# A two-layer attention trunk with its layer loop written out: layer 0 reads the input itself, and the final norm moves into the last merge stage

## The reference, cut to what matters

```python
def rms_norm(x, w):
    y = x * rsqrt(mean(x * x, axis=-1) + EPS)
    return y * w

def mixer_layer(x, ...):
    h = rms_norm(x, norm_w)
    u = h @ w_in                       # 1024 -> 6144 columns: q, k, v, gates of two branches, merge gates
    ...                                # differential attention (o_da), stick-breaking attention (o_sb)
    y_da = (rms_norm(o_da, subln_w) * (1.0 - lam_init)) * silu(gd)
    y_sb = o_sb * silu(gs)
    merged = sigmoid(ga) * (y_da @ w_proj_da) + sigmoid(gb) * (y_sb @ w_proj_sb)
    return x + merged @ w_out, (kd, vd, ks, vs)

for l in range(2):
    x, rows = mixer_layer(x, ...)
y = rms_norm(x, final_norm_w)          # outputs: y and the new k and v rows of each layer
```

## Time and profile before

| what | us |
|---|---|
| median of 3 runs (lowest, highest) | 3524.44 (3505.21, 3526.84) |
| the profiled execution | 3517.19 |
| its span, first to last instruction | 3515.4 |
| PE busy | 2985.0 (85% of the span) |
| DVE busy / ACT busy | 1558.3 / 992.9 |
| mean granted PE clock, as a share of full speed | 0.924 |

### The profile page before, as it was taken

One profiled execution on the slowest core, in us unless ns is written; L12 is line 12 of the kernel. 1 busy time (PEld: TensorE's weight loads), 2 busy tenths in 40 slices (PEclk: granted clock), 3 DMA queues, 4 the chain that ended last, 5 costly groups with the idle time before them and its releaser, 6 DMA issues. The chain is left out here.

```text
span 3515.4 us, 52769 instructions
## 1 busy us (share of the span) xinstructions
PE 2985.0 (85%) x19664; PEld 2303.6 (66%) x19664; DVE 1558.3 (44%) x2399; ACT 992.9 (28%) x1751; POOL 0.2 (0%) x4
## 2 busy tenths in 40 slices
PE   5999999787787877769889999997877788786896
PEld 4888888555555555558668888884555555555685
DVE  4522110355664746564263222105646557455543
ACT  3101111343443524320030011113525344343211
POOL 0000000000000000000000000000000000000000
PEclk9999999898998989879989999998979889897998
DMA  4322221664544554354242222116555554553444
GB/s 174 141 96 88 79 95 51 218 215 166 184 168 164 206 187 153 110 200 139 93 153 102 96 95 96 72 48 233 207 177 172 202 180 162 190 183 117 170 139 160
DMA packets 288645, 516.62 MB, mean 147 GB/s; under 512 B 19040, under 2 KB 89824, under 8 KB 282208
## 3 DMA queue, kind: packets, MB, share of 16 engines
q1 hardware_dynamic: 288432, 513.72, 42.0%
HBM read 433.43 MB, written 84.93 MB: 147 GB/s over the span
## 5 line engine op out<-in xcount | busy, mean ns | idle before, releaser
L185 PE MATMUL A_acc<-A_w_hi,A_ht_hi 128*128 128x512 f32 x1728 | 675.2, 391 | 5.9 <-DVE A_w_lo L326 5.9
L185 PE MATMUL A_acc<-A_w_hi,A_ht_lo 128*128 128x512 f32 x1728 | 673.5, 390 | 0.0
L185 PE MATMUL A_acc<-A_w_lo,A_ht_hi 128*128 128x512 f32 x1728 | 673.3, 390 | 0.0
L719 PE MATMUL B_tr<-ident,B_k 128*128 128x128 f32 x2048 | 325.9, 296 | 123.9 <-DVE B_ckt L954 111.5
L719 PEld LDWEIGHTS B_tr<-ident,B_k 128*128 128x128 f32 x2048 | 232.7, 148 | 270.5 <-DVE B_ckt L954 138.8
L185 PEld LDWEIGHTS A_acc<-A_w_hi,A_ht_hi 128*128 128x128 f32 x1728 | 325.1, 188 | 73.8 <-issue 6.6
L185 PEld LDWEIGHTS A_acc<-A_w_hi,A_ht_lo 128*128 128x128 f32 x1728 | 325.0, 188 | 67.9
L185 PEld LDWEIGHTS A_acc<-A_w_lo,A_ht_hi 128*128 128x128 f32 x1728 | 325.2, 188 | 67.1
L801 PE MATMUL B_ov<-B_nat_v,B_wt 128*128 128x64 f32 (+1 forms) x1728 | 239.9, 297 | 0.0
L954 DVE COPY B_ckt<-B_tr 128x512 f32<-128x512 f32 x272 | 186.8, 687 | 104.2 <-PE B_tr L719 103.9
L801 PEld LDWEIGHTS B_ov<-B_nat_v,B_wt 128*128 128x128 f32 x1728 | 232.5, 215 | 0.0
(11 more groups left out here) (140 smaller groups left out, 3559.5 us busy)
## 6 DMA issues: line engine op xcount, KB each, us to landing
B_k<-in_cache_da_k SPq DMA_DIRECT2D x64, 1024.0 KB, 5.4
B_v<-in_cache_da_v SPq DMA_DIRECT2D x64, 1024.0 KB, 9.9
B_k<-in_cache_sb_k SPq DMA_DIRECT2D x64, 1024.0 KB, 5.2
B_v<-in_cache_sb_v SPq DMA_DIRECT2D x64, 1024.0 KB, 9.5
A_w_raw<-in_w_in SPq DMA_DIRECT2D x48, 1024.0 KB, 5.3
tmp_gates<-A_stage SPq DMA_DIRECT2D x72, 256.0 KB, 2.0
D_gate<-tmp_gates SPq DMA_DIRECT2D x72, 256.0 KB, 3.5
D_w_raw<-in_w_merge SPq DMA_DIRECT2D x32, 512.0 KB, 6.3
```

The lines of the kernel that those rows point to most:

```text
L185: last = nc.tensor.matmul(acc[:, i % RING, :], h[:, k, t * P:(t + 1) * P], w[:, b, k, :], start=(n == 0), stop=(n == 3 * KC - 1))
L719: last = nc.tensor.transpose(tr[:, r % 2, j * P:(j + 1) * P], block_, ident[:, :])
```

## The change

The diff with the renaming of tiles and semaphores (from "A_" to f"A{l}_" and so on, in all three phases) left out:

```diff
 def end_phase(nc, sems):
-    nums = [s.num for s in sems]
-    assert max(nums) - min(nums) == len(nums) - 1
-    nc.gpsimd.sem_clear(range(min(nums), max(nums) + 1))
+    nums = sorted(s.num for s in sems)
+    first = nums[0]
+    for num, after in zip(nums, nums[1:] + [None]):
+        if after != num + 1:
+            nc.gpsimd.sem_clear(range(first, num + 1))
+            first = after
     nc.all_engine_barrier()

+def x_of(dram, l):
+    return dram["x_all"] if l == 0 else dram["x"]

 # phase_project, SP
-                sp.wait_ge(const["x_here0"], 16)
                 for t in range(2):
-                    sp.dma_start(x_in[:, t, :], dram["x"][t]).then_inc(x_sems[t], 16)
+                    sp.dma_start(x_in[:, t, :], x_of(dram, l)[t]).then_inc(x_sems[t], 16)
                 load_w(0, True)
-                sp.wait_ge(const["x_here1"], 16)
                 for t in range(2, NT):
                     sp.wait_ge(S["hn_ready"], t - 1)
-                    sp.dma_start(x_in[:, t % 2, :], dram["x"][t]).then_inc(x_sems[t % 2], 16)
+                    sp.dma_start(x_in[:, t % 2, :], x_of(dram, l)[t]).then_inc(x_sems[t % 2], 16)

 # phase_merge
+        final = l == DEPTH - 1
+        fw = sbuf(f"D{l}_fw", [P, D])
+        fsq = sbuf(f"D{l}_fsq", [P, D])
+        fstats = sbuf(f"D{l}_fstats", [P, 4])
 # SP
                 def load_x(i):
                     done(sp, "x_ready", i - 1)
-                    sp.dma_start(x_in[:, :], dram["x"][i - 1]).then_inc(S["in1"], 16)
+                    sp.dma_start(x_in[:, :], x_of(dram, l)[i - 1]).then_inc(S["in1"], 16)
                 def store_x(i):
-                    sp.wait_ge(S["x_ready"], i)
-                    sp.dma_start(dram["x"][i - 1], x_out[:, :]).then_inc(S["x_stored"], 16)
+                    if final:
+                        sp.wait_ge(S["y_out"], i)
+                        sp.dma_start(dram["y"][i - 1], x_out[:, :]).then_inc(S["x_stored"], 16)
+                    else:
+                        sp.wait_ge(S["x_ready"], i)
+                        sp.dma_start(dram["x"][i - 1], x_out[:, :]).then_inc(S["x_stored"], 16)
                         ...
+                if final:
+                    sp.dma_start(fw[:, :], dram["final_norm_w"]).then_inc(S["fw_in"], 16)
                 load_branches(3)
                 load_gates(2)
 # ACT
+                def final_norm(i):
+                    act.wait_ge(S["x_ready"], i)
+                    done(act, "fsq_done", i - 1)
+                    nc.scalar.activation(fsq[:, :], x_out[:, :], ACT.Square, accum_out=fstats[:, 0:1]).then_inc(S["fsq_done"], 1)
+                    act.wait_ge(S["fvar_ready"], i)
+                    nc.scalar.activation(fstats[:, 2:3], fstats[:, 1:2], ACT.Sqrt).then_inc(S["fsd_ready"], 1)
                 with act.Fori(2, NT) as i:
                     root(i + 1)
                     y_part(i + 1)
                     m_part(i)
+                    if final:
+                        final_norm(i - 1)
                 m_part(NT)
+                if final:
+                    final_norm(NT - 1)
+                    final_norm(NT)
 # DVE
+                def final_norm(i):
+                    dve.wait_ge(S["fsq_done"], i)
+                    nc.vector.tensor_scalar(fstats[:, 1:2], fstats[:, 0:1], 1.0 / D, EPS, ALU.mult, ALU.add).then_inc(S["fvar_ready"], 1)
+                    dve.wait_ge(S["fsd_ready"], i)
+                    nc.vector.reciprocal(fstats[:, 3:4], fstats[:, 2:3]).then_inc(S["f_step"], 1)
+                    dve.wait_ge(S["f_step"], i)
+                    nc.vector.scalar_tensor_tensor(out=x_out[:, :], in0=x_out[:, :], scalar=fstats[:, 3:4], in1=fw[:, :],
+                                                   op0=ALU.mult, op1=ALU.mult).then_inc(S["y_out"], 1)
+                if final:
+                    dve.wait_ge(S["fw_in"], 16)
                 with dve.Fori(2, NT) as i:
                     ...
                     m_part(i)
+                    if final:
+                        final_norm(i - 1)
                 merge(NT)
                 add_x(NT - 1)
                 m_part(NT)
+                if final:
+                    final_norm(NT - 1)
                 add_x(NT)
+                if final:
+                    final_norm(NT)

-def phase_final(nc, dram, const):
-    ...

 # build
-                for part, tiles in enumerate((slice(0, 2), slice(2, NT))):
-                    sp.dma_start(dram["x"][tiles].rearrange("t p c -> (t p) c"),
-                                 dram["x_all"][tiles].rearrange("t p c -> (t p) c")).then_inc(const[f"x_here{part}"], 16)
                 for name in loads:
                     sp.dma_start(const[name][:, :], dram["c_" + name]).then_inc(const["loaded"], 16)

-        with nc.Fori(0, DEPTH) as l:
+        for l in range(DEPTH):
             phase_project(nc, l, dram, const)
             phase_attention(nc, l, dram, const)
             phase_merge(nc, l, dram, const)
-        phase_final(nc, dram, const)
```

More of the change, by code:

```diff
@@ L88, in phase_project @@
                  "st0", "st1", "st2", "st3", "st4", "st5"]
-        S = {n: scope.enter_context(nc.semaphore("A_" + n)) for n in names}
+        S = {n: scope.enter_context(nc.semaphore(f"A{l}_" + n)) for n in names}
         stored = [S[f"st{i}"] for i in range(RING)]
[L91 to L104, removed]
+        ht_hi = sbuf(f"A{l}_ht_hi", [P, KC, NT * P], F32R)
+        ht_lo = sbuf(f"A{l}_ht_lo", [P, KC, NT * P], F32R)
+        w_raw = sbuf(f"A{l}_w_raw", [P, 2, KC // 2 * BLK])
+        w_hi = sbuf(f"A{l}_w_hi", [P, 2, KC, BLK], F32R)
+        w_lo = sbuf(f"A{l}_w_lo", [P, 2, KC, BLK], F32R)
+        stage = sbuf(f"A{l}_stage", [P, RING, BLK])
+        x_in = sbuf(f"A{l}_x_in", [P, 2, D_MODEL])
+        nw = sbuf(f"A{l}_nw", [P, D_MODEL])
+        hn = sbuf(f"A{l}_hn", [P, D_MODEL])
+        rope_t = sbuf(f"A{l}_rope_t", [P, NT, 2 * HEAD_DIM])
+        small = sbuf(f"A{l}_small", [P, 8])
+        lamq = sbuf(f"A{l}_lamq", [P, 4, HEAD_DIM])
+        lamp = sbuf(f"A{l}_lamp", [P, 2, HEAD_DIM])
+        rope_s = sbuf(f"A{l}_rope_s", [P, 2, BLK])
         t_cos, t_sin = rope_s[:, 0, :], rope_s[:, 1, :]
-        tr = psum("A_tr", [P, 2, BLK])
-        acc = psum("A_acc", [P, RING, BLK])
+        tr = psum(f"A{l}_tr", [P, 2, BLK])
+        acc = psum(f"A{l}_acc", [P, RING, BLK])
         ident, nlam, lam_c = const["ident"], const["nlam"], const["lam_c"]
@@ L517, in phase_attention @@
                  "k0", "k1", "k2", "k3", "v0", "v1", "v2", "v3"]
[L518 to L525, removed]
@@ L548, in phase_attention @@
[L548 to L551, removed]
+        S = {n: scope.enter_context(nc.semaphore(f"B{l}_" + n)) for n in names}
+        nat = [sbuf(f"B{l}_nat_q", [P, NP_T, P]), sbuf(f"B{l}_nat_k", [P, NP_T, P])]
+        nat_v = [sbuf(f"B{l}_nat_v{a}", [P, NP_T, P]) for a in range(2)]
+        qkt = [sbuf(f"B{l}_qt", [P, SEQ]), sbuf(f"B{l}_kt", [P, SEQ])]
+        fun = sbuf(f"B{l}_fun", [P, 2, SEQ])
@@ new lines, in phase_attention @@
+        ew = [sbuf(f"B{l}_ew{p}", [P, 2, SEQ]) for p in range(2)]
+        surv = sbuf(f"B{l}_surv", [P, 2, SEQ])
+        wt = sbuf(f"B{l}_wt", [P, 2, SEQ])
+        stats = [sbuf(f"B{l}_stats{p}", [P, 8]) for p in range(2)]
+        o_st = sbuf(f"B{l}_o_st", [P, 4, P])
+        k_in = [sbuf(f"B{l}_k{s}", [P, PIECE, BLK]) for s in range(4)]
+        v_in = [sbuf(f"B{l}_v{s}", [P, PIECE, BLK]) for s in range(4)]
+        ckt = [sbuf(f"B{l}_ckt{p}", [P, NC, BLK]) for p in range(2)]
+        ckn = sbuf(f"B{l}_ckn", [P, NC, DEC_SEQ])
@@ new lines, in phase_attention @@
+        k_new = sbuf(f"B{l}_kn", [DEC_SEQ, BLK])
+        v_new = sbuf(f"B{l}_vn", [DEC_SEQ, BLK])
+        qz = [sbuf(f"B{l}_qz{a}", [P, B, NC, 2 * DEC_SEQ]) for a in range(2)]
+        qzc = sbuf(f"B{l}_qzc", [P, NC, 2 * DEC_SEQ])
+        q_nat = fun
+        probs = [sbuf(f"B{l}_probs{p}", [P, KEYS]) for p in range(2)]
+        cfun = sbuf(f"B{l}_cfun", [P, 2, BLK])
+        csig = sbuf(f"B{l}_csig", [P, 2, BLK])
+        csurv = sbuf(f"B{l}_csurv", [P, BLK + 1])
+        pt = sbuf(f"B{l}_pt", [P, KT + 1, P])
@@ L552, in phase_attention @@
+        cstats = [sbuf(f"B{l}_cstats{p}", [P, 4]) for p in range(2)]
+        osc = sbuf(f"B{l}_osc", [P, P])
+        co_st = sbuf(f"B{l}_co_st", [HD, 2, P])
+        masks_r = sbuf(f"B{l}_masks_r", [P, MASKS], F32R)
+        sc = psum(f"B{l}_sc", [P, 2, SEQ])
+        csc = psum(f"B{l}_csc", [P, BLK])
+        tr = psum(f"B{l}_tr", [P, 2, BLK])
+        ov = psum(f"B{l}_ov", [P, BLK])
         ident, nlam, own, pair_sum, lam_row = (const[k] for k in ("ident", "nlam", "own", "pair_sum", "lam_row"))
@@ L1068, in phase_merge @@
                  "y_ready", "y_tr", "y_hi", "y_lo", "proj_done", "m_ready", "m_tr", "m_hi", "m_lo", "out_done",
-                 "x_ready", "sub_scaled", "norm_step", "merge_step", "x_stored"]
-        S = {n: scope.enter_context(nc.semaphore("D_" + n)) for n in names}
-        w_raw = sbuf("D_w_raw", [P, RAW, D])
```

(20 more changed lines are left out.)

74 lines of the change are left out of this document (4 added, 70 removed).

## The result

| what | before | after |
|---|---|---|
| median of 10 runs (lowest, highest), us | 3519.47 (3505.21, 3526.84) | 3482.26 (3467.43, 3496.59) |
| ratio, 95% interval | | 0.9898 (0.9875 to 0.9921) |
| the profiled execution, its span, us | 3517.19, 3515.4 | 3491.46, 3489.7 |

The kernel is 1.0% faster. The forecast was 3484, and a gain of 36.8 us; the medians differ by 37.2.

What follows compares the result with a forecast made beforehand. PE was taken to bound the long stretches, leaving gains at start, turn and end: 11.0 + 3.1 + 24.2 - 1.5 = 36.8 us off, giving 3480.4 or 3487.6 by starting point; middle 3484 us, range 3467 to 3500.

Steps and rivals of the forecast that it cites:

- Start of layer 0: Kernel start: without the two DRAM copies and their waits, PE's first product comes 11.0 us earlier; ends 1.3 and 11.4.
- Turn between the layers: Layer 0 to layer 1: without the taken jump, SP's gap is 0.9 us, not 4.0; 3.1 saved, ends 0 and 3.1.
- End: Behind the last add_x: phase_final's loads and serial tiles go, one tile's norm and store remain; 24.2 us saved, low end 22.5.
- Norm in the merge loop: Last merge loop: the added norm delays sub_norm 2.2 us within 4.6 of slack; cost 0, ends 0 and 22 us.
- Load of the final norm's weights: Last merge phase: the 512 KB load delays tile 3's branch loads and so PE; 1.5 us added, ends 0.4 and 2.5.
- The step that failed: Attention phase: it keeps its steps and its loop over h, so its change was costed at nothing.
- the third rival: Pair and merge loops: longer code makes PE stall at 18 jumps back, 3.517 us each, 63 in all; 3547 us, chance 0.04.
- the three pieces: Savings at layer 0's start, the turn between layers and the end, forecast as 11.0, 3.1 and 24.2 us.
- this very sign of being wrong: Attention phase: the prediction counts as wrong if its length changes by more than a few us.

Runs made afterwards that it cites:

- e5: Changed kernel plus two DRAM copies ahead of the constants to a scratch tensor nobody reads, with no load waiting for them; single execution 3499.84 us.
- e12: The kernel before, unaltered, run once more for a second trace; single execution 3527.29 us.
- e7: Changed kernel with seven more chained, unused DVE products of 512 columns behind each final norm; single execution 3530.26 us.
- e6: Changed kernel with the final norm's weight load moved behind tile 3's branch and tile 2's gate loads, its wait moved to the product; single execution 3479.11 us.
- e1: Kernel before with only the layer loop written out; copies, waits and separate final norm stay; ratio to before 1.0001 (0.9988 to 1.0014).
- e4: The changed kernel run once more, for a second trace; ratio to before 0.9895 (0.9878 to 0.9913).
- e10: Changed kernel with 24 unused transposes (48 instructions) ahead of PE's attention loop in layer 1; ratio to before 0.9895 (0.9876 to 0.9915).
- e9: Changed kernel with 8 unused transposes (16 instructions) ahead of PE's attention loop in layer 1; single execution 3488.06 us.
- e11: Changed kernel with reordered first loads in each layer, later final-norm weight load and 24 unused transposes before layer 1's attention loop; ratio to before 0.9879 (0.9859 to 0.99).

## Why the prediction was right

**The whole.** 3484 us forecast, 3482.26 measured; 36.8 us of gain forecast, 37.2 measured. Three terms were right in kind and two of them too small, beyond the upper ends that I gave, and a term costed at nothing ate the difference. That the sum came so close is in part luck. So is the starting point: 3484 is the middle between two values of before that lie 7 us apart, and the same 36.8 us off the median of ten runs would be 3482.7.

**Start of layer 0**, 11.0 us: 13.0 (26.20 against 39.16), beyond the upper end I gave. The constants cost nothing; without the copies beside them their five issues were quicker too (3.43 for the next phase's first issue, 4.16 forecast), and from there to the first product it took 22.8 us, less than the 23.6 that I took from layer 1. That the copies hold SP and the waits cost nothing is shown by e5. The poor end of this term went into the range as 9 us, which no row gives; the end stated with the term was 1.3.

**Turn between the layers**, 3.1 us: 3.8 to 4.4 against the first trace of before, and 0.8 more against e12. The branch rows give the 3.1 (4.0 to 0.9); the rest is again the shorter way from first issue to first product, 22.85 us for 23.56. Writing the loop out did two things to this stretch: it took away the jump, and it made the layer number, which had been in a register, a constant. From the first issue of the layer to that of the weights SP now takes 2.9 us in place of 3.3, which is a part of that rest.

**End**, 24.2 us: 24.3, each step as written (3484.78 + 1.28 - 3482.94 = 3.12 for 3.16, landing 2.3).

**Norm in the merge loop**, 0 us: right. `sub_norm` starts 2.0 us later against `add_x` than before, 2.2 forecast; e7 shows where the cover ends.

**Load of the final norm's weights**, 1.5 us: 1.3 at DVE by e6. PE's wait for tile 3 was to be near 9 us; it was 7.2 and 8.4 in the two traces, for 7.65 before. The load did cost PE some 2 us there, but the wait that it was added to had become 2 us shorter with the loop written out, and the two nearly cancel.

**The step that failed** is the sentence "The attention phase, in which PE waits now and then, keeps its steps and its loop over h, so I leave it at nothing", and with it the limit of the third rival to the pair loop and the merge loop. Neither of those stalled. PE has no gap in the stretch of the merge loop shown with e7, nor in this one of the pair loop of layer 1 in the changed kernel:

```profile
1800.00:2300.00 500.00, 500.00 (x2212) 414.11 (x2211) 122.32 (x141) 69.19 (x70) 0.00 (x0) 1.00 0.26 93
```

The attention loop already stopped at its jumps, and there the new place of layer 1's code added a second stop in trips 2 to 4. Directly these are 6.9 us in the trace after (2.20 + 2.11 + 2.58), and about 9 us in the first halves of the trips; layer 1's attention came out 6 to 8 us longer than before in e1, e4 and their like. Taking 6 to 9 from the 41 us of the three pieces leaves 32 to 35, beside 36.6 and 37.2 measured: within the intervals, 6 to 8 us to either side. The prediction named this very sign of being wrong, a change of the attention phase by more than a few us, and it came: 17.7 us in the first pair of traces, 6 to 8 of them beyond scatter. What stays open is why e10, without the second stop, has no shorter phase in its one trace.

On the Trainium skill's rule (Runtime: NRT & Kernel Launch, section on instruction fetch), by which a jump out of the present window stalls and fetching goes on block by block: e9 and e10 agree with it, as the stop moves with the stream and not with the work. It is there named for the jump alone; here the second stop, some 10 to 25 instructions behind the loop's head, took another 0.6 to 4.4 us.

## What to carry to other kernels

Look at what stands in a queue ahead of a kernel's first useful load, and at what follows its last product: that is where the 37 us of 3519 lay, while the projection and the steady merge loop had no gap to give. Terms added up from marks like these came within 2 us of what they measured, but a phase whose clock goes up and down scatters by up to 18 us; judge such a change by marks in the trace beside medians of many runs, never by two spans. When code is written out, look at the heads of the loops that are left: here it was the loop whose jumps already cost something that got a further stop.

## What the runs showed of the hardware that I had not expected

- A gap of 3.0 us a trip in an otherwise full PE loop cost 5.0 us, as the granted clock of the loop fell from 1.00 to 0.93 (e7).
- Behind a jump back, PE stopped a second time at a fixed place of its instruction stream, for 0.6 to 4.4 us, as long as that place lay some 10 to 25 instructions behind the loop's head (after and e1 to e9); with the loop 48 instructions further on it did not (e10, e11). PE went on about 5 us after the trip's first matmul wherever it had stopped.
- Two DRAM-to-DRAM copies ahead in SP's queue held the issue of a 128 KB load for 10.3 us, and for 11.5 where nothing waited for them (e5), and made the issues between them slower, 0.44 to 0.71 us each in place of 0.39 to 0.43.
